# Triangular inverses of the RWKV chunks in packed 32x32 blocks instead of 64x64 ones

## The reference, cut to what matters

```
def _rwkv7_step(state, inp):
    r, w, k, v, kk, kka = inp
    sa = jnp.einsum('dbhvk,dbhk->dbhv', state, kk)
    state = state * w[..., None, :] - sa[..., :, None] * kka[..., None, :] + v[..., :, None] * k[..., None, :]
    y = jnp.einsum('dbhvk,dbhk->dbhv', state, r)
    return state, y
```

## Time and profile before

| | us |
|---|---|
| three runs, median (lowest to highest) | 1295.57 (1292.97 to 1296.23) |
| the profiled execution | 1297.45 |
| its span in the trace | 1295.4 |
| PE busy in the span | 1230.7 (95%) |
| PEld, DVE, ACT, POOL busy | 1153.2, 586.2, 617.9, 896.1 |

### The profile page before, as it was taken

How to read it: one execution, slowest core, us unless ns; L and a number is a source line. 1 busy time by engine, 2 the same in 40 slices (tenths; PEclk the granted TensorE clock), 3 DMA queues, 4 the chain that set the end, 5 groups by cost and what they waited for, 6 DMA issues and landing times.

```text
span 1295.4 us, 27192 instructions
## 1 busy us (share of the span) xinstructions
PE 1230.7 (95%) x11566; PEld 1153.2 (89%) x11566; DVE 586.2 (45%) x1057; ACT 617.9 (48%) x969; POOL 896.1 (69%) x689
## 2 busy tenths in 40 slices
PE   6999799999999999998899999999899988999997
PEld 6999689899998899997899998989898977999996
DVE  2533546742652222224545334458977444432333
ACT  5665434736744444445544445675322014544443
POOL 5988245686986999994799994867400013999992
PEclk9999999999999999999999999989999998999998
DMA  6555134454565556563555655434100022665561
GB/s 247 191 165 179 50 93 139 145 180 146 184 220 165 178 182 190 183 188 115 158 191 184 191 182 194 154 121 157 36 3 3 4 68 66 196 189 185 188 186 66
DMA packets 53256, 189.81 MB, mean 147 GB/s; under 512 B 6160, under 2 KB 7312, under 8 KB 53008
## 3 DMA queue, kind: packets, MB, share of 16 engines
q1 hardware_dynamic: 50256, 181.95, 43.9%
q10 hardware_dynamic: 2880, 6.12, 1.4%
HBM read 187.00 MB, written 1.05 MB: 145 GB/s over the span
## 4 chain that ended last, share of the span: by engine, by line
PE 83%; DVE 9%; ACT 5%; DMA 2%; issue 1%; POOL 0%; DVEq 0%; ACTq 0%
PE product L500 16%; PE product L502 16%; PE product L501 16%; PE bank L557 6%; PE bank L559 6%; PE bank L558 6%; PE product L1036 3%; PE bank L1036 3%; ACT weight_hi L2242 1%; PE product L587 1%; PE product L631 1%; PE bank L500 1%; DVE arena L1504 1%; PE bank L868 1%; PE bank L501 1%
## 5 line engine op out<-in xcount | busy, mean ns | idle before, releaser
L477 POOL TENSOR_TENSOR weight_lo<-raw_ring,weight_hi 128x512 fp32r<-128x512 f32 x684 | 890.6, 1335 | 375.3 <-ACT weight_hi L2242 344.1
L2242 ACT ACTIVATE weight_hi<-raw_ring 128x1024 fp32r<-128x1024 f32 x338 | 356.1, 1059 | 413.4 <-DMA raw_ring<-in_ffn_gu 108.1
L500 PE MATMUL product<-operand_B_hi,weight_hi 128*128 128x256 f32 x1104 | 312.3, 283 | 4.6 <-POOL weight_lo L477 4.6
L502 PE MATMUL product<-operand_B_hi,weight_lo 128*128 128x256 f32 x1104 | 311.3, 282 | 0.0
L501 PE MATMUL product<-operand_B_lo,weight_hi 128*128 128x256 f32 x1104 | 310.8, 282 | 0.0
L500 PE MATMUL product<-operand_A_hi,weight_hi 128*128 128x256 f32 x840 | 242.5, 289 | 14.2 <-DVE weight_lo L1353 10.8
L502 PE MATMUL product<-operand_A_hi,weight_lo 128*128 128x256 f32 x840 | 238.4, 284 | 0.0
L501 PE MATMUL product<-operand_A_lo,weight_hi 128*128 128x256 f32 x840 | 238.3, 284 | 0.0
L500 PEld LDWEIGHTS product<-operand_B_hi,weight_hi 128*128 128x128 f32 x1104 | 208.1, 188 | 7.9 <-issue 3.2
L501 PEld LDWEIGHTS product<-operand_B_lo,weight_hi 128*128 128x128 f32 x1104 | 207.9, 188 | 3.2
L502 PEld LDWEIGHTS product<-operand_B_hi,weight_lo 128*128 128x128 f32 x1104 | 207.9, 188 | 0.0
(11 more groups left out here) (355 smaller groups left out, 1571.1 us busy)
## 6 DMA issues: line engine op xcount, KB each, us to landing
raw_ring<-in_w_in SPq DMA_DIRECT2D x107, 512.0 KB, 3.5
raw_ring<-in_ffn_gu SPq DMA_DIRECT2D x88, 512.0 KB, 3.5
raw_ring<-in_ffn_down SPq DMA_DIRECT2D x44, 512.0 KB, 3.5
raw_ring<-in_w_mlp_up SPq DMA_DIRECT2D x32, 512.0 KB, 4.2
raw_ring<-in_w_mlp_down SPq DMA_DIRECT2D x32, 512.0 KB, 4.2
raw_ring<-in_w_out SPq DMA_DIRECT2D x16, 512.0 KB, 4.2
raw_ring<-in_w_branch_c SPq DMA_DIRECT2D x8, 512.0 KB, 3.4
raw_ring<-in_w_branch_a SPq DMA_DIRECT2D x8, 512.0 KB, 3.4
```

Of the source, the lines that this page charges most:

```text
L477: last = k.nc.gpsimd.tensor_tensor(k.wlo[:, slot, part], k.raw[:, slot, part], k.whi[:, slot, part].bitcast(F32), ALU.subtract)
L500: mm(ps, w_hi, op.hi[:, b, :], start=b == 0, stop=False)
L502: return mm(ps, w_lo, op.hi[:, b, :], start=False, stop=b == blocks - 1)
L2242: k.nc.scalar.activation(k.whi[:, slot, 0:w], k.raw[:, slot, 0:w], ACT.Copy).then_inc(k.s["hi_ready"], 1)
```

## The change

The 64x64 system is cut into two 32x32 blocks on its diagonal and the block between them. The diagonal blocks of all 16 systems now lie as 8 units of 32 columns on four quarters of the partitions (two per head). Levels 1 to 4 stay inside these blocks and are done by `quarters`, 32 matmuls of 32x32 by 32 columns; level 5 joins the two halves with `between_halves`, 16 such matmuls. Only the transpose `tt` is multiplied; the inverse `tc` is made from it by VectorE's transpose in 32x32 blocks. `first_products` gets `left_products`, which makes one orientation only and packs it by halves, with the half that starts the recursion in columns 0 to 31. The finished parts are copied into `ttc`, which GpSimd has zeroed before: the diagonal blocks by ScalarE in four copies per step (`diagonal_halves`), the block between by VectorE in four copies per step. The masks of the levels are 32 wide. In the attention softmax the scores are negated, so that the minimum replaces maximum and negation, and the exponential gets scale -1.

```diff
@@ gpsimd_program
     pool.wait_ge(k.s["cbaq_made"], 2)
+    pool.wait_ge(k.s["cb_made"], 1)
+    for j in range(NRC):
+        k.nc.gpsimd.memset(k.ttc[j], 0.0).then_inc(k.s["tt_zero"], 1)
     low_parts(before_rwkv, k.total)
@@ tensor_program
+    def left_products(j):
+
+        bank = k.lane[j % 2][1]
+        for u in range(8):
+            lhs, rhs = feature(B_, j)(u), feature(A_, j)(u)
+            ahead = 0 if u < 4 else 1
+            for i in (ahead, 1 - ahead):
+                for head in (0, HD):
+                    rows, out = slice(head, head + HD), slice(head + i * HC, head + (i + 1) * HC)
+                    own, other = slice(i * HC, (i + 1) * HC), slice((1 - i) * HC, (2 - i) * HC)
+                    if i == 0 and ahead == 0:
+                        mm(bank[out, u * RC:(u + 1) * RC], lhs[rows, own], rhs[rows, :], start=True, stop=True)
+                    else:
+                        last = mm(bank[out, u * RC:u * RC + HC], lhs[rows, own], rhs[rows, own], start=True, stop=True)
+                        if i == ahead:
+                            last = mm(bank[out, u * RC + HC:(u + 1) * RC], lhs[rows, own], rhs[rows, other],
+                                      start=True, stop=True)
+        return last
+
+    def quarters(bank, lhs, rhs):
+
+        for u in range(8):
+            for q in range(4):
+                rows = slice(q * HC, (q + 1) * HC)
+                last = mm(bank[rows, u * HC:(u + 1) * HC], lhs[rows, u, 0:HC], rhs[rows, u, 0:HC], start=True, stop=True)
+        return last
+
+    def between_halves(bank, lhs, rhs, forward):
+
+        for u in range(4):
+            for q in range(4):
+                n = u if (q % 2 == 0) == forward else u + 4
+                rows, out = slice(q * HC, (q + 1) * HC), slice((q ^ 1) * HC, ((q ^ 1) + 1) * HC)
+                last = mm(bank[out, n * HC:(n + 1) * HC], lhs[rows, n, :], rhs[rows, n, :], start=True, stop=True)
+        return last
 ...
-            pe.wait_ge(s["tt_ev"], 9 + j % 2)
-        per_unit(lane[0], feature(A_, j), feature(B_, j)).then_inc(s["prod_mm"], 1)
-        per_unit(lane[1], feature(B_, j), feature(A_, j)).then_inc(s["prod_mm"], 1)
+            pe.wait_ge(s["tt_off"], 4 * (j - 1))
+        left_products(j).then_inc(s["prod_mm"], 1)
         per_unit(lane[2], feature(B_, j), feature(Q_, j)).then_inc(s["prod_mm"], 1)
 ...
     def level_left(j, level):
 ...
-        per_unit(bank, of(k.nt[j % 2]), of(k.tc[j % 2])).then_inc(s["u_mm"], 1)
+        if level < 5:
+            quarters(bank, k.nt[j % 2], k.tc[j % 2]).then_inc(s["u_mm"], 1)
+        else:
+            between_halves(bank, k.nt[j % 2][:, :, HC:RC], k.tc[j % 2], True).then_inc(s["u_mm"], 1)
     def level_both(j, level):
 ...
-        if level < 5:
-            per_unit(lane[2], of(k.ttc[j]), of(k.uc[j % 2])).then_inc(s["t_mm"], 1)
-        per_unit(lane[0], of(k.uc[j % 2]), of(k.ttc[j])).then_inc(s["tt_mm"], 1)
+            quarters(bank, k.uc[j % 2], k.tt[j % 2]).then_inc(s["tt_mm"], 1)
+        else:
+            between_halves(bank, k.uc[j % 2], k.tt[j % 2], False).then_inc(s["tt_mm"], 1)
@@ half_row
-            pe.wait_ge(s["tt_ev"], nth(3, 5, 5))
+            pe.wait_ge(s["tt_off"], 4 * NRC)
@@ vector_program, attention_scores
-        nv.scalar_tensor_tensor(sc, k.score_bank[:], HD ** -0.5, wide(k.att_mask), ALU.mult,
-                                ALU.add).then_inc(s["s_ev"], 1)
+        nv.scalar_tensor_tensor(sc, k.score_bank[:], -(HD ** -0.5), wide(k.att_mask), ALU.mult,
+                                ALU.subtract).then_inc(s["s_ev"], 1)
         v.wait_ge(s["s_ev"], h + 1)
-        st.do(nv.tensor_reduce(sm[:, 64 + 2 * h:66 + 2 * h], sc.rearrange("p (i t) -> p i t", i=2), AX_X, ALU.max))
-        st.settle()
-        nv.tensor_scalar(sm[:, 80 + 2 * h:82 + 2 * h], sm[:, 64 + 2 * h:66 + 2 * h], -1.0, None,
-                         ALU.mult).then_inc(s["s_red"], 1)
+        nv.tensor_reduce(sm[:, 80 + 2 * h:82 + 2 * h], sc.rearrange("p (i t) -> p i t", i=2), AX_X,
+                         ALU.min).then_inc(s["s_red"], 1)
@@ vector_program, the inverse
+    def turned(j, level):
+
+        v.wait_ge(s["tt_ev"], nth(j, level))
+        nv.transpose(k.tc[j % 2].rearrange("p u t -> p (u t)"),
+                     k.tt[j % 2].rearrange("p u t -> p (u t)")).then_inc(s["t_ev"], 1)
     def first_products(j):
 ...
-        masked(tc, lane[0], 0).then_inc(s["la_ev"], 1)
-        v.wait_ge(s["prod_mm"], products_before(j) + 2)
-        masked(ttc, lane[1], 0, turned=True).then_inc(s["nt_ev"], 1)
-        v.wait_ge(s["la_ev"], j + 1)
-        nv.tensor_tensor(tc, tc, stack8, ALU.add).then_inc(s["tc_first"], 1)
-        v.wait_ge(s["nt_ev"], j + 1)
-        nv.tensor_tensor(ttc, ttc, stack8, ALU.add).then_inc(s["ttc_first"], 1)
-        v.wait_ge(s["prod_mm"], products_before(j) + 3)
+        if j >= 2:
+            v.wait_ge(s["tt_diag"], 4 * (j - 1))
+        nv.tensor_tensor(by_way(tt), by_way(units(lane[1])[:, :, 0:HC]), half_mask(0), ALU.mult).then_inc(s["nt_ev"], 1)
+        v.wait_ge(s["nt_ev"], j + 1)
+        nv.tensor_tensor(by_way(tt), by_way(tt), half_mask(5), ALU.add).then_inc(s["tt_ev"], 1)
+        turned(j, 0)
+        v.wait_ge(s["prod_mm"], products_before(j) + 2)
         masked(k.zaqb[j], lane[2], BEFORE_OR_SAME).then_inc(s["qb_ev"], 1)
 ...
     def level_left(j, level):
 ...
-        masked(k.uc[j % 2], k.lane[j % 2][1], level).then_inc(s["u_ev"], 1)
+        if level < 5:
+            nv.tensor_tensor(by_way(k.uc[j % 2]), by_way(bank), half_mask(level), ALU.mult).then_inc(s["u_ev"], 1)
+        else:
+            nv.tensor_copy(k.uc[j % 2], bank).then_inc(s["u_ev"], 1)
     def level_both(j, level):
 ...
-            nv.tensor_tensor(k.tc[j % 2], units(lane[2]), k.tc[j % 2], ALU.add).then_inc(s["t_ev"], 1)
-        nv.tensor_tensor(k.ttc[j], units(lane[0]), k.ttc[j], ALU.add).then_inc(s["tt_ev"], 1)
+            nv.tensor_tensor(tt, bank, tt, ALU.add).then_inc(s["tt_ev"], 1)
+            turned(j, level)
+            return
+        v.wait_ge(s["tt_zero"], NRC)
+        for head in (0, HD):
+            for rows, n, cols in ((slice(head, head + HC), slice(0, AB), slice(HC, RC)),
+                                  (slice(head + HC, head + HD), slice(AB, 8), slice(0, HC))):
+                nv.tensor_copy(k.ttc[j][rows, n, cols], bank[rows, n, :]).then_inc(s["tt_off"], 1)
@@ scalar_program
+    def diagonal_halves(j):
+
+        act.wait_ge(s["tt_zero"], NRC)
+        act.wait_ge(s["tt_ev"], 10 * (j // 2) + 8 + j % 2 + 1)
+        for q in range(4):
+            rows, cols = slice(q * HC, (q + 1) * HC), slice((q % 2) * HC, (q % 2 + 1) * HC)
+            f(k.ttc[j][rows, :, cols], k.tt[j % 2][rows, :, :], ACT.Copy).then_inc(s["tt_diag"], 1)
 ...
     for level in range(1, 6):
         attention(4 + 2 * level)
+        if level == 5:
+            diagonal_halves(0)
+            diagonal_halves(1)
         attention(5 + 2 * level)
 ...
     right_side(0)
     solution(0)
+    diagonal_halves(2)
+    diagonal_halves(3)
     right_side(1)
     solution(1)
```

More of the change, by code:

```diff
@@ L45 @@
 RC = 64
+HC = RC // 2
 NRC = T // RC
@@ L403, in allocate @@
     k.levels = k.masks.rearrange("p (d m t) -> p d m t", d=2, m=8)
-    k.nt, k.tc, k.uc = ([units(9760 + 1536 * lane + 512 * n) for lane in range(2)] for n in range(3))
+    k.levels_half = k.masks.rearrange("p (d m t) -> p d m t", d=2, m=16)
+    half_units = lambda start: region(start, 8, HC)
+    k.nt = [units(9760 + 1536 * lane) for lane in range(2)]
+    k.tc, k.uc, k.tt = ([half_units(9760 + 1536 * lane + 512 + 256 * n) for lane in range(2)] for n in range(3))
     k.ttc, k.zaac, k.zaqc = ([units((12832, 15904, 18976, 6144)[j] + 512 * n) for j in range(NRC)] for n in range(3))
@@ L1061, in second_products @@
         lane = k.lane[j % 2]
-        pe.wait_ge(s["la_ev"], j + 1)
         per_unit(lane[0], feature(C_, j), feature(A_, j)).then_inc(s["prod_mm"], 1)
@@ L1127, in solve @@
         pe.wait_ge(s["x_ev"], j + 1)
-        pe.wait_ge(s["tt_ev"], nth(j, 5, 5))
+        pe.wait_ge(s["tt_diag"], 4 * (j + 1))
+        pe.wait_ge(s["tt_off"], 4 * (j + 1))
         per_unit(k.chain_bank, of(k.ttc[j]), of(k.xs)).then_inc(s["sa_mm"], 1)
@@ L2042, in masked, with half_mask, nth @@
         return nv.tensor_tensor(by_way(dst), by_way(units(bank)), m.unsqueeze(2).to_broadcast([P, 2, AB, RC]), ALU.mult)
[L2044 to L2045 removed]
+    products_before = lambda j: 12 * (j // 2) + 2 * (j % 2)
+    products_between = lambda j: 12 * (j // 2) + 4 + 3 * (j % 2)
+    half_bank = lambda bank: bank[:, 0:8 * HC].rearrange("p (u t) -> p u t", u=8)
+    def half_mask(n):
+        return k.levels_half[:, :, n, :].unsqueeze(2).to_broadcast([P, 2, AB, HC])
+    def nth(j, level):
+        return 10 * (j // 2) + 2 * level + j % 2 + 1
+    def turned(j, level):
+        v.wait_ge(s["tt_ev"], nth(j, level))
+        nv.transpose(k.tc[j % 2].rearrange("p u t -> p (u t)"),
```

(13 more changed lines are left out.)

45 lines of the change are left out of this document (16 added, 29 removed).

## The result

| | before | after |
|---|---|---|
| median of 8 runs each (lowest to highest), us | 1295.55 (1292.97 to 1297.54) | 1304.92 (1299.87 to 1306.85) |
| span of the profiled execution, us | 1295.4 | 1302.7 |
| mean granted clock of TensorE | 0.986 | 0.965 |
| PE busy, us (MATMUL records) | 1230.7 (11566) | 1220.3 (12142) |

The account below looks back on a forecast made before the run. PE was taken to bound the levels through the count and pitch of its matmuls; gains of 0.7, 5.2, 0.7, 0.3, 1.75 and 4.8 less losses of 0.55 and 1.3 gave 11.6 us less, 1284.0 us, range 1277 to 1303.

Parts of the forecast that it names:

- First products: Stretch from 917 to 934 us: 0.3 us credited for VectorE's narrower operations, besides 0.7 less through `left_products`.
- Levels of pair (0, 1): Recursion levels of the first two steps: 1.3 us gained in each of four levels, 5.2 together, and 0.7 in level 5.
- I take 1.01: Estimated PE time of one `quarters` in us: 32 matmuls at 31.7 ns, from columns streamed plus a remainder.
- both of its bounds: Limits for one `quarters`: 1.87 us if nothing shrinks, 0.6 us if records follow at less than 10 ns.
- My own sign: Check in PE's timeline: 1.0 us per `quarters` expected; 1.6 or more proves the per-record cost rival, 0.6 the greater-overlap rival.
- better still: Rival, chance 0.08: `quarters` overlap more, 0.6 us each, VectorE's chain then limits the levels; 1278 us.
- those couples: Reading of PE's records: two start less than 10 ns apart, about 50 ns between couples, taken as time for columns.
- Pair (2, 3): Steps 2 and 3: 1.75 us less before `from_state(0)`, 4.8 less from there to `solve(1)`.
- The clock: Rival, chance 0.07: PE's more and longer waits lower its clock; six falls cost 11 us, giving 1295.
- A record costs what it costs: Rival, chance 0.18: a record's cost does not depend on its size, 1.87 us per 64 records; 1313 us.
- the wait of the values of head 6: Level-5 attention of pair (0, 1): ScalarE's copies delay probabilities, so PE's values wait 0.55 us.
- The wait at `half_row(0)`: End of pair (2, 3): PE waits for all eight VectorE copies, 1.3 us late (0.3 to 2.0).

Follow-up runs that it names:

- e8: Kernel before plus one burst of 512 unread 32x32 matmuls by 32 columns (1,024 records) ahead of the levels; 1326.5 us, ratio 1.0239.
- e6: Kernel before with each matmul of the levels issued as two of 32 columns, same 64x64 weights, twice the records; 1347.41 us, ratio 1.0404.
- e2: Changed kernel plus 25 filler matmuls that compute nothing wanted, put where PE waits; 1297.60 us, ratio 1.0018.
- e1: Kernel before, 64x64 products kept, only the inverse made from its transpose by VectorE instead of multiplied; 1288.41 us, ratio 0.9952.
- e3: Changed kernel with each `quarters` as 16 matmuls of 64 columns, half the records, part of the inverse not computed; 1274.0 us, ratio 0.984.
- e5: Kernel of e1 with other PE work moved before products that need VectorE's result, and VectorE's state turn later; 1278.58 us, ratio 0.9871.
- e9: Changed kernel with the same reorderings as e5; 1296.1 us, ratio 1.0008.

## Why the prediction was wrong

The starts of the same groups on PE, both traces, against the terms as I summed them:

| | before | after | measured | forecast |
|---|---|---|---|---|
| first `level_left(0)` | 936.88 | 935.29 | -1.6 | -0.7 |
| scores of level 5 | 973.16 | 974.23 | +1.1 | -5.9 |
| `from_state(0)` | 1004.41 | 1006.24 | +1.8 | -8.1 |
| `to_state(1)` | 1036.63 | 1044.32 | +7.7 | -11.6 |
| end of the span | 1295.4 | 1302.7 | +7.3 | -11.6 |

- **First products: right, a little better.** VectorE's additions took 0.42 us (beside POOL's memsets, 1.92 us for the four) and 0.72 (beside its low parts), against up to 1.75 before, for twice the width.
- **Levels of pair (0, 1): this failed**, by 7.9 us (from the first row to the second 5.2 less was forecast, and it became 2.7 more). The step that failed is "I take 1.01" for a `quarters`, and more exactly that it, and both of its bounds, came from how long a record occupies the array. The array is faster than I took (0.61 us), and that was of no use: the mean over the stream is what counts. My own sign would have misled, as it had 0.6 us for a `quarters` prove "better still", 1278 us. In e8 it is 3.83 us per 128 records, 30 ns per record, 1.9 us per `quarters`, my upper bound by another mechanism. A row of that size stood there, 29.2 ns per record in the earlier trace rows, though no run shows that the supply set it in the kernel before. With the same 29 ns in e6 for half the columns, my lowering of it had no ground. I explained by columns; those couples show how close two starts can be, not how many can come.
- **Pair (2, 3): failed for the same reason**, by 9.4 us between `from_state(0)` and `to_state(1)`. It has no scores and values in which blocks could catch up, and 6.05 of its 9.6 us of stops lie in that stretch; from 1004 to 1037 the mean clock is 0.66, before it was 0.95. Where before PE ran 350 records in the 10 us from 1015 to 1025, it now runs 298, and is busy 6.06 us with them: waits for VectorE (0.41 before each `level_left` of step 3) delay a stream that had nothing to spare.
- **The clock: a rival by itself, in truth a consequence.** I gave it 0.07 and 1295 us, counting waits of 0.15 to 0.5. It fell behind stops of 0.89 and 1.74 us, to 0.50 from 945 to 970, and in the burst of e8 behind the first stop of 2.03. The fillers gave back 7 us, their own work included. Its cost is also visible in `from_state(0)`, which took 3.68 us for 64 records instead of the 2.82 before.
- **"A record costs what it costs" had the right sign** and 0.18, partly by luck: its time of 1313 is 8 us too high, and what costs is not the start of a record but its supply. The Trainium skill states a floor of about 25 ns between starts in "TensorE: Matmul & The Clock Gate", section "Wait — 56ns, not 53.3ns?". The 1302 worked out from it lies 3 us below the result, but the floor is not what acts: starts 9.5 ns apart in the trace after, and 160 records in 1.55 us in e8, contradict it for matmuls in four corners.
- **What acts has a page too, with the opposite conclusion.** "Runtime: NRT & Kernel Launch", section "Instruction fetch mechanics", of the Trainium skill says that instructions come in blocks of 16 KiB (256 instructions), and that crossing a block is mostly hidden because dispatch is slower than the refill. The size agrees with this case (128 records and their loads per 16 KB packet); that it is hidden does not: PE stands idle 1.5 to 2.2 us per block in e8.
- **Small terms that were right.** Transpose 0.446 us for 256 columns (taken 0.42). ScalarE's eight copies 3.46 us (3.2); the wait of the values of head 6 is hidden by the slow clock after, and 0.72 in e2 (0.55 taken). VectorE's copies 0.287 each (0.29). The wait at `half_row(0)` as put:

```profile
977.85 3.46 ACT L2777 ACTIVATE arena<-arena 32x256 f32<-32x256 f32 x8
1042.73 0.50 PE L564 MATMUL bank<-weight_hi,operand_A_hi 128*128 128x512 f32 x1 [1.27 <-DVE arena L2142]
```

Open: what sets the lengths of the three parts of a cycle, and how the loss splits between stops and clock, since the clock falls behind stops. The range to 1303 missed the time by 2 us.

## What to carry to other kernels

Count the instructions of a stretch before cutting matmuls into smaller ones: in a long stream of small float32 matmuls here a record had better be worth 30 ns of array time on the mean, or the engine waits for its instructions and its clock can fall too. Drop products (e1) or widen them (e3 prices it) rather than shorten them. When a change adds a hop over another engine, move independent work behind it in the same edit: the transposes alone gave 6.5 us (e1), the order around them 9.8 more (e5).

## What the runs showed of the hardware

- Four 32x32 corners side by side start records 9.5 ns apart at full clock (the changed kernel) and at most 15 at half (e8), but not longer than their stock lasts: 160 records of the burst before its first stop.
- 128 records with their weight loads are one packet of 16 KB on the instruction queue, one per 3.4 to 4.2 us in the stretches that wait for it (e8, e9, the changed kernel). PE restarts 1.2 to 1.6 us after a packet has landed, in all 41 stops of four kernels. Neither the order of the work nor the clock changed that much.
- The clock fell behind short waits too: e3 idles 1.0 us in a level of 6.0, in waits of 0.45 and 0.58, keeps 1.00 from 935 to 960 and has 0.58 from 960 to 965; the changed kernel, with stops of 0.89 and 1.74, loses it at 945. The same wait of 2.45 us before `from_state(0)` is followed by 0.66 in the kernel before, and by 1.00 in e1 (from 940 to 1010). The length of the last wait alone doesn't tell.
